# Sparse-attention projections of a four-layer trunk: VectorE takes each unit out before its next weight split, GpSimd makes half of the compression copies, the rotary partner copies go to SyncE's queue

## The reference, cut to what matters

```python
q, kc, vc, ks, vs, kw, vw, gates = jnp.split(h @ w_in, splits, axis=-1)
q  = apply_rope(q);  ks = apply_rope(ks);  kw = apply_rope(kw)
gates = jax.nn.sigmoid(gates)

def compress(t, pe, w1, w2):              # 31 blocks of 32 positions, stride 16
    blocks = t[:, blk_idx] + pe[:, None, :]
    blocks = ...reshape(B, n_cmp, G, CMP_LEN * dk)
    return jax.nn.gelu(blocks @ w1) @ w2
k_cmp = apply_rope(compress(kc, cmp_pe[0], cmp_w1[0], cmp_w2[0]))
v_cmp = compress(vc, cmp_pe[1], cmp_w1[1], cmp_w2[1])
# scores of q against k_cmp, softmax, times v_cmp; then the selected and the window branch
```

## Time and profile before

| | us |
|---|---|
| three runs | 2951.76, 2953.64, 2955.32 (median 2953.64) |
| the profiled execution's own time | 2953.68 |
| its span | 2951.9 |
| PE busy in the span | 2858.2 (97%) |
| VectorE, ACT, GpSimd busy | 1376.6, 983.6, 474.3 |
| mean granted clock of TensorE | 0.99 |
| NSA projections, unit 3 to the last compressed softmax | about 706 to 869 of the span |

### The profile page before, as it was taken

One profiled execution on the slowest core, in us unless ns is written; L12 is line 12 of the kernel. 1 busy time (PEld: TensorE's weight loads), 2 busy tenths in 40 slices (PEclk: granted clock), 3 DMA queues, 4 the chain that ended last, 5 costly groups with the idle time before them and its releaser, 6 DMA issues. The chain is left out here.

```text
span 2951.9 us, 37772 instructions
## 1 busy us (share of the span) xinstructions
PE 2858.2 (97%) x14556; PEld 2353.7 (80%) x14556; DVE 1376.6 (47%) x1827; ACT 983.6 (33%) x1571; POOL 474.3 (16%) x363
## 2 busy tenths in 40 slices
PE   7999999998999999999999997999999999999998
PEld 5888888887876688888877875888888788888887
DVE  4464543335557754333445555443334465443333
ACT  4322432225145543222322323332223433332222
POOL 0021122100111212221011221022210012022210
PEclk9999999999999999999999998999999999999999
DMA  4323233333510023333232221233332332233331
GB/s 146 93 85 94 70 107 95 96 100 107 142 44 1 1 65 107 99 90 101 85 100 79 85 67 55 86 93 97 93 98 90 103 90 86 79 93 99 98 93 59
DMA packets 459669, 256.07 MB, mean 87 GB/s; under 512 B 9632, under 2 KB 447632, under 8 KB 459424
## 3 DMA queue, kind: packets, MB, share of 16 engines
q1 hardware_dynamic: 455488, 246.50, 28.5%
q10 hardware_dynamic: 3456, 5.77, 0.7%
q0 software_dynamic: 608, 2.16, 0.2%
HBM read 248.11 MB, written 2.10 MB: 85 GB/s over the span
## 5 line engine op out<-in xcount | busy, mean ns | idle before, releaser
L1443 DVE TENSOR_TENSOR w_lo<-w_raw,w_hi 128x1024 fp32r<-128x1024 f32 x461 | 626.0, 1359 | 943.9 <-ACT w_hi L1058 943.4
L478 PE MATMUL acc<-a_hi,w_hi 128*128 128x512 f32 x2264 | 890.1, 393 | 8.3 <-DVE y_lo L1899 5.1
L480 PE MATMUL acc<-a_hi,w_lo 128*128 128x512 f32 x2264 | 880.0, 389 | 0.0
L479 PE MATMUL acc<-a_lo,w_hi 128*128 128x512 f32 x2072 | 807.0, 389 | 0.0
L1058 ACT ACTIVATE w_hi<-w_raw 128x1024 fp32r<-128x1024 f32 x461 | 483.5, 1050 | 521.6 <-PE acc L480 462.5
L478 PEld LDWEIGHTS acc<-a_hi,w_hi 128*128 128x128 f32 x2264 | 426.2, 188 | 101.1 <-issue 12.8
L480 PEld LDWEIGHTS acc<-a_hi,w_lo 128*128 128x128 f32 x2264 | 425.6, 188 | 88.4
L479 PEld LDWEIGHTS acc<-a_lo,w_hi 128*128 128x128 f32 x2072 | 389.7, 188 | 79.8 <-issue 1.4
L480 PE MATMUL acc<-hid_hi,w_lo 128*128 128x512 f32 (+1 forms) x704 | 264.5, 376 | 0.0
L479 PE MATMUL acc<-hid_lo,w_hi 128*128 128x512 f32 (+1 forms) x704 | 264.5, 376 | 0.0
L478 PE MATMUL acc<-hid_hi,w_hi 128*128 128x512 f32 (+1 forms) x704 | 264.5, 376 | 0.0
(11 more groups left out here) (302 smaller groups left out, 3484.7 us busy)
## 6 DMA issues: line engine op xcount, KB each, us to landing
w_raw<-ffn_w_gate SPq DMA_DIRECT2D x88, 512.0 KB, 3.8
w_raw<-ffn_w_up SPq DMA_DIRECT2D x88, 512.0 KB, 3.8
w_raw<-gm_w_in SPq DMA_DIRECT2D x64, 512.0 KB, 4.0
w_raw<-ffn_w_down SPq DMA_DIRECT2D x64, 512.0 KB, 3.8
w_raw<-ret_w_in SPq DMA_DIRECT2D x48, 512.0 KB, 3.8
w_raw<-gm_w_out SPq DMA_DIRECT2D x32, 512.0 KB, 3.7
w_raw<-ffn_w_down SPq DMA_DIRECT2D x32, 384.0 KB, 3.3
w_raw<-nsa_w_in SPq DMA_DIRECT2D x21, 512.0 KB, 3.9
```

The source lines that it names most:

```text
L478: pe.matmul(o_bank, lhs_hi, rhs_hi, start=start, stop=False)
L479: pe.matmul(o_bank, lhs_hi, rhs_lo, start=False, stop=False)
L480: return pe.matmul(o_bank, lhs_lo, rhs_hi, start=False, stop=stop)
L1443: dve.tensor_tensor(w_lo[:, slot, :, :], w_raw[:, slot, :, :], w_hi[:, slot, :, :].bitcast(f32), ALU.subtract).then_inc(lo_done, 1)
```

## The change

Seven edits, all in the NSA projections.

1. **VectorE**: in step u, `ahead` (`w_lo` of unit u+3) moves from the front of the step to behind the drain of unit u.
2. **Copies shared**: ACT makes two of the four copies of each compression input, those that change the half of the partitions; GpSimd makes the other two (new semaphore `kc_half`). VectorE's drains and `stage` wait for both.
3. **Partner DMAs**: the four DMAs of each roped unit move from ACT's queue to SyncE's, ahead of the weight load of seven units later; the last three stand after all loads of the projections.
4. `value_out` moves from after unit 16 to after unit 17, and its result from PSUM bank `tr` 0 to `tr` 1.
5. ACT's `block_values` moves from step 17 to step 18.
6. The wait for `vblk` moves to the first transposition of the compressed probabilities, the other two disappear.
7. GpSimd waits for its own eight copies before the first rotary addition.

```diff
@@ SyncE
                 if L["kind"] == 1:
+                    def partner(u):
+
+                        earlier = [w for w in range(u) if NSA_UNITS[w][1] in ROPED and w % 2 == u % 2]
+                        sp.wait_ge(acc_free, L["o_in"] + u + 1)
+                        if earlier:
+                            sp.wait_ge(n_rope, nth(earlier[-1], ROPED) + 1)
+                        for quarter in range(4):
+                            to, of = 32 * quarter, 32 * (quarter ^ 1)
+                            sp.dma_start(work[to:to + 32, 4 + u % 2, :], work[of:of + 32, u % 2, :]).then_inc([rot_even, rot_odd][u % 2], 16)
+
                     for u, (c0, _) in enumerate(NSA_UNITS):
+                        if u >= 7 and NSA_UNITS[u - 7][1] in ROPED:
+                            partner(u - 7)
                         load(L["n_in"] + u, (L["n_in"] + u) % SLOTS, nsa_w_in[z, :, c0:c0 + P], DT)
...
+                    for u in range(len(NSA_UNITS) - 7, len(NSA_UNITS)):
+                        if NSA_UNITS[u][1] in ROPED:
+                            partner(u)
@@ PE
-                            last = pe.matmul(tr[:, 0, g * HD:(g + 1) * HD], h1v[:, hh, g, :], w2[:, 1, hh, 0:HD], start=hh == 0, stop=hh == 1)
+                            last = pe.matmul(tr[:, 1, g * HD:(g + 1) * HD], h1v[:, hh, g, :], w2[:, 1, hh, 0:HD], start=hh == 0, stop=hh == 1)
...
                     pe.wait_ge(pc_done, c + 1)
                     wait(pe, pc_t, c)
+                    if c == 0:
+                        pe.wait_ge(vblk_done, 4)
...
-                    elif i == 1:
-                        pe.wait_ge(vblk_done, 4)
...
-                    if u == 16:
+                    if u == 17:
                         value_out()
@@ ACT
-                        if u == 17:
+                        if u == 18:
                             block_values()
...
-                        if kind in ROPED:
-
-                            earlier = [w for w in range(u) if NSA_UNITS[w][1] in ROPED and w % 2 == u % 2]
-                            act.wait_ge(acc_free, o0 + u + 1)
-                            if earlier:
-                                act.wait_ge(n_rope, nth(earlier[-1], ROPED) + 1)
-                            for quarter in range(4):
-                                to, of = 32 * quarter, 32 * (quarter ^ 1)
-                                act.dma_start(work[to:to + 32, 4 + u % 2, :], work[of:of + 32, u % 2, :]).then_inc([rot_even, rot_odd][u % 2], 16)
...
                             for side in range(2):
-                                for l2 in range(2):
-                                    last = act.activation(kc2[l2 * HD:(l2 + 1) * HD, t // 2, 2 * (t % 2) + side, 0:SEQ - l2],
-                                                          work[side * HD:(side + 1) * HD, u % 2, l2:SEQ], ACT.Copy)
+                                l2 = 1 - side
+                                last = act.activation(kc2[l2 * HD:(l2 + 1) * HD, t // 2, 2 * (t % 2) + side, 0:SEQ - l2],
+                                                      work[side * HD:(side + 1) * HD, u % 2, l2:SEQ], ACT.Copy)
                             last.then_inc(kc_done, 1)
@@ VectorE
                     dve.wait_ge(kc_done, 2 * (br + 1))
+                    dve.wait_ge(kc_half, 4 * (br + 1))
...
                         if u >= 2:
-                            ahead(n0, 0, 1, u)
                             if u in CMP_AFTER:
                                 stage(CMP_AFTER.index(u))
...
                                 dve.wait_ge(kc_done, nth(u - 2, ("kc", "vc")) + 1)
+                                dve.wait_ge(kc_half, 2 * nth(u - 2, ("kc", "vc")) + 2)
...
                             dve.tensor_tensor(dst, src, R[:, :], ALU.mult).then_inc(acc_free, 1)
+                        if u >= 2:
+                            ahead(n0, 0, 1, u)
@@ GpSimd
+                        if kind in ("kc", "vc"):
+
+                            t = nth(u, ("kc", "vc"))
+                            pool.wait_ge(acc_free, L["o_in"] + u + 1)
+                            pool.wait_ge(n_zero, 2)
+                            for side in range(2):
+                                wait(pool, kc_half, 2 * t + side)
+                                pool.tensor_copy(kc2[side * HD:(side + 1) * HD, t // 2, 2 * (t % 2) + side, 0:SEQ - side],
+                                                 work[side * HD:(side + 1) * HD, u % 2, side:SEQ]).then_inc(kc_half, 1)
                         if kind not in ROPED:
                             continue
+                        if u == NSA_Q0:
+                            pool.wait_ge(kc_half, 8)
```

More of the change, by code:

```diff
@@ L320, in build @@
             o_sum r_mean_mm r_mu_ready ro_cen ro_sq ro_csum r_var_mm r_var_rd r_root r_sd_ready ry_done rg_done y_hi_done y_lo_done
-            n_tab_in n_zero rot_even rot_odd rope_t n_rope kd_dup kc_done nv_tr nv_done sig_done gt_done mask_r
+            n_tab_in n_zero rot_even rot_odd rope_t n_rope kd_dup kc_done kc_half nv_tr nv_done sig_done gt_done mask_r
             stg_ready cmp_mm h1_done kcmp_mm kcmp_x kcmp_rot kcmp_done vcmp_mm vblk_done
@@ L336, in build @@
          o_sum, r_mean_mm, r_mu_ready, ro_cen, ro_sq, ro_csum, r_var_mm, r_var_rd, r_root, r_sd_ready, ry_done, rg_done, y_hi_done, y_lo_done,
-         n_tab_in, n_zero, rot_even, rot_odd, rope_t, n_rope, kd_dup, kc_done, nv_tr, nv_done, sig_done, gt_done, mask_r,
+         n_tab_in, n_zero, rot_even, rot_odd, rope_t, n_rope, kd_dup, kc_done, kc_half, nv_tr, nv_done, sig_done, gt_done, mask_r,
          stg_ready, cmp_mm, h1_done, kcmp_mm, kcmp_x, kcmp_rot, kcmp_done, vcmp_mm, vblk_done,
@@ L822, in cmp_values @@
                     pe.wait_ge(acc_free, o0 + (last_unit + 1 if c == CH - 1 else 18 + c))
-                    if c == 0:
-                        pe.wait_ge(vblk_done, 4)
                     for hp in range(H_NSA // 2):
@@ L1258, in block_values @@
                             act.activation(vblk[32 * r:32 * r + 32, :, HD * r:HD * (r + 1)],
-                                           tr[32 * r:32 * r + 32, 0, 0:G_NSA * HD].rearrange("p (g d) -> p g d", g=G_NSA), ACT.Copy).then_inc(vblk_done, 1)
+                                           tr[32 * r:32 * r + 32, 1, 0:G_NSA * HD].rearrange("p (g d) -> p g d", g=G_NSA), ACT.Copy).then_inc(vblk_done, 1)
                     def cmp_exp(c):
```

## The result

The changed kernel takes 2925.02 us (median of 4 runs, 2924.18 to 2926.34) beside 2952.70 for the kernel before (4 runs). The direction and the places were right; the size was off by 3.5 us.

What follows compares the result with a forecast made beforehand. PE, busy 97%, bounds the kernel; only its waits in the NSA projections and the slow clock behind them can be won. Terms 13.3 + 3.5 + 7.4 = 24.2 us from 2953.68 give 2929.5 us, range 2926.5 to 2936.5.

Steps and rivals of the forecast that it cites:

- The start: NSA projections, unit 5 to first compression: shared copies and drain first (edits 1, 2, 7) remove waits and slow clock, 13.3 us.
- The walk: Step-by-step timing of ACT, GpSimd and VectorE at the start: `stage` 0 ends at 723.7, 0.9 us before PE needs it.
- The short waits for `stage`: PE's later waits in the projections: moving partner DMAs to SyncE (edit 3) removes them, 3.5 us.
- `value_out`, 7.4 us: After unit 16: edits 4 to 6 remove the gelu wait and slow clock over `value_out` and unit 17, 7.4 us.
- `block_values` and the softmax at nothing: Before the first transposition: moved `block_values` and `vblk` wait cost nothing, bounded by 0 and about 1 us.
- The rule against the partners: SyncE's queue: ring order holds partners of units 5, 8, 11 behind w1, landing in 8.8 us; 2.4 us lost at most.
- the last one of the sum: Whole program: 24.2 us off the profiled 2953.68 gives 2929.5, everything after the projections moving ahead as a whole.
- the signs of being wrong: A copy over 1.4 us, partner landings over 8 us, or new PE idle over 2 us between 720 and 880.
- Slow copies: Rival, start: GpSimd copies above 1.43 us each delay `stage` 0; at 2.54 the time is 2936.2; chance 0.10.
- Late partners: Rival, SyncE's queue: some partners late behind w1, first softmax 1 us late; 20.8 us won, 2932.9; chance 0.11.
- the queue as the bound: Rival, SyncE's queue: partner groups landing in over 8 us set the pace; at 14, 2965.5; chance 0.03.
- Waits that only move: Rival, attention proper: PE idles the same later, on drain, duplicate or weights; 2953; chance 0.03.

Runs made afterwards that it cites:

- the second profile: The changed kernel run and profiled once more with no edit: 2927.20 us (4 runs), ratio 0.9912 to the kernel before.
- the fourteen: Profiles of this study, two of either kernel and one of each variant; the same code behind the projections' changed stretch took 2079.3 to 2083.7 us.
- the second one: The kernel before run and profiled once more with no edit: 2952.46 us against 2952.49 of its neighbours.
- The second four runs: The changed kernel run again with no edit: 2927.20 us, ratio 0.9912 (0.9897 to 0.9927) to the kernel before.

## Why the prediction was right or wrong, point by point

**The start, 13.3 us: right.** From the drain of unit 0 to the second compression it was 745.66 - 712.37 = 33.29 before and is 732.97 - 713.18 = 19.79 after, 13.5 won. The walk put `stage` 0 at 722.7; it came at 723.50, which is 722.7 on the old scale, since this execution runs 0.81 later. What set it was ACT: the split of unit 7 waited for `w_hi`, which ended at 722.32, 721.5 on the old scale, where the walk had 721.4. GpSimd's copies took 0.64 to 1.08 us each where the walk had used 1.27, and VectorE's first two splits took 1.58 and 1.55 instead of 1.23, but neither was what `stage` waited for last.

**The short waits for `stage`, 3.5 us: mis-sized, 4.3 measured.** From the second compression to the end of unit 16 it was 817.88 - 745.66 = 72.22 before and 800.89 - 732.97 = 67.92 after. I took the idle time of the rows. It counts from the modelled end of the last matmul, 0.39 after its start, though the next can start 0.23 after; each of the three waits is thus about 0.16 longer than its row. A fourth delay of 0.15 has no idle in the rows at all (767.31 behind 766.93), and two compressions took 2.02 us where they take 1.94 after. Timeline of PE before:

```profile
759.82 2.02 PE L771 MATMUL st<-stg,w1k_b 128*128 128x124 f32 x16 [1.33 <-DVE stg L1617]
...
766.93 0.39 PE L480 MATMUL acc<-a_hi,w_lo 128*128 128x512 f32 x1
767.31 2.02 PE L771 MATMUL st<-stg,w1k_b 128*128 128x124 f32 x16
...
781.55 2.02 PE L771 MATMUL st<-stg,w1v_a 128*128 128x124 f32 x16 [0.83 <-issue]
...
803.28 2.02 PE L771 MATMUL st<-stg,w1v_b 128*128 128x124 f32 x16 [1.33 <-DVE stg L1617]
```

For the 9.8 us wait I had used starts, and there the term was right. This is the one error of method in the terms. I also credited edit 3 with this term; the runs show that edit 1 alone does it as well.

**`value_out`, 7.4 us: right in the sum, wrong as a part.** From the end of unit 16 (0.23 behind the start of its last matmul) to the scores it was 832.55 - 817.88 = 14.67 and is 808.15 - 800.89 = 7.26, 7.4 won. But alone the edits give nothing in S, and with edits 1 to 3 in place they are worth about the bare 1.7 us where the clock holds, 5.6 where it doesn't. The 7.4 belong to all the edits together, which the sentence on the gelu's extra unit didn't say.

**`block_values` and the softmax at nothing, up to 1 us lost: right.** The first transposition follows unit 18 with no idle.

**The rule against the partners: no loss, and the wait behind w1 is there.** Landings were 1.9 to 5.0 us (up to 5.5 in the second profile). The long ones are the three groups that the rule named, those of units 5, 8 and 11 behind a w1 load, with 3.0 to 5.0 us; all others landed in 1.9 to 2.0. Timeline of SyncE after:

```profile
744.28 0.61 SPq L457 DMA_DIRECT2D w1v_a<-nsa_cmp_w  x1
746.64 2.42 SPq L447 DMA_DIRECT2D work<-work  x4
...
764.31 0.60 SPq L457 DMA_DIRECT2D w1v_b<-nsa_cmp_w  x1
767.12 2.65 SPq L447 DMA_DIRECT2D work<-work  x4
```

The two w1 parts took 6.8 and 6.9 us to land, and the first partner DMAs behind them 4.6 and 4.1. So w1 and partner landed together both times, at 751.1 and 751.2, and at 771.2 and 771.2 (counted from the start of each issue; within 0.4 us in the second profile). Behind w1k_b (724.02 and 8.1) the first partner (726.32 and 4.5) landed at 730.8, 1.3 us ahead of it. But before, on ACT's own queue, the first partners of units 7 and 10 did the same behind the same loads (issued at 753.89 and 775.65 and landed after 4.9 and 4.6, with w1 landing at 758.8 and 780.3 as well). So the delay comes with either queue, and whether queue order or taking turns makes it, these runs don't tell. The estimate of 8.8 us failed in adding a partner's own 2.4 us behind the end of the w1 load, and in taking the longest w1 landing. The 2.4 us put into the range weren't needed.

**The step that failed** is the last one of the sum, where 24.2 was set against one profiled execution and the rest of the program was said to move "as a whole". It does, but its own time varies. That execution's 2083.2 us behind S are 1.6 above the median of the fourteen (2081.6), and after's first profile, with 2080.6, lay 1.0 below it. In times of the whole program the base was 1.2 too high, 2953.68 where 48 runs have 2952.5. A smaller miss is the term of the short waits, 3.5 where 4.3 were measured, most of the 1.3 us by which S did better than the sum. Inside S 25.5 us were won against this profile, and 26.4 against the second one, which took 10.4 us instead of 9.5 from the first compression to the second. With 8 runs, 2925.9, the gain is 26.6, and 0.6 us lies outside the range: of the 3.6 us between forecast and time, 1.2 are the base, 1.3 to 2.2 the gain in S beyond 24.2 (by the one profile before or the other), and up to 1.1 stay open. The second four runs alone, 2927.2, lie inside the range, so how far the first four came out below it is partly chance. The low end lay 3 us below the forecast, for slow stretches and small gaps inside the projections, of which 1.3 were used; what the untouched code varies by, about 2 us to either side, was not in it.

**The rivals.** None of the signs of being wrong appeared: GpSimd's copies took 1.08 us at most (two in 2.16), landings 5.5, and no new idle of over 2 us stands on PE. Slow copies: not so, but the cover was 2.7 us smaller than reckoned. Late partners and the queue as the bound: not so. Waits that only move: true of edits 4 to 6 by themselves, not of the whole.

## What to carry to other kernels

Where two engines hand work to and fro, put first what frees the other one, and judge the edits as a set: here single edits won 11.4, 4.9, 10.0 and 0.0 us in S, and taking the order, the partners or `value_out` out of the whole cost 10.9, 2.0, and 1.7 or more. Measure a wait from start to start against what back-to-back instructions take; the idle column understates it a little each time. And before a forecast of under 1% is bounded, look how much the untouched part of the program varies between executions.

## What the runs showed of the hardware that I had not expected

GpSimd and VectorE slow each other. `stage` (four instructions of 128x124) takes 1.05 us with GpSimd idle and 2.09 when a rotary addition runs beside it (five of the eight in the kernel after); in the kernel before the two never met. Timelines of VectorE and GpSimd after:

```profile
784.08 2.09 DVE L1622 TENSOR_SCALAR stg<-kc,lnp 128x124 f32<-128x124 f32 x4
...
789.52 1.05 DVE L1622 TENSOR_SCALAR stg<-kc,lnp 128x124 f32<-128x124 f32 x4
```

```profile
784.25 1.32 POOL L1981 TENSOR_TENSOR nq<-work 128x512 f32<-128x512 f32 x1 [5.96 <-DVE work L1706]
```

Which of the two loses differs. In the kernel after, the first split took 1.58 us instead of 1.23 and the copy beside it lost nothing, and at the second both lost, 0.3 and 0.9 us. With the copies made two or three times, all splits but one kept 1.21 or 1.22 and the copies lost 0.9 to 1.0 for each. The Trainium skill (GPSIMD Engine Reference, Key points) says that GpSimd shares its SBUF interfaces with VectorE and contends with VectorE instructions that have two SBUF inputs or run in a two-port mode. The times of the split, which has two such inputs, agree (1.58 against 1.23); in which mode `stage` runs no row shows.

TensorE's clock fell to half behind a wait of 2.35 us in one kernel and of 1.70 in another, and stayed whole behind 1.52 in a third and 2.71 in a fourth (the copies made twice, compression 2.02 us). In after without edit 1 it fell at 818 us with no idle ahead of it. Which it is can differ between executions of one program, as the end of the attention shows. Behind S the two profiles of the kernel before differ by 2.2 us, those of after by 1.4, and in after without 4 to 6 the fall cost some 3.7 us on top of the wait (5.6 less 1.7, less the 0.16 of the idle column).
